# Modulation weights laid out with one output per partition, multiplied and summed by VectorE alone

## The reference

```python
cond = jax.nn.silu(c)                                # first block, c is [1, 1024]
mod = (cond @ ada_w[i] + ada_b[i])[:, None, :]       # 2 layers, ada_w[i] is [1024, 6144]
sh1, sc1, g1, sh2, sc2, g2 = jnp.split(mod, N_MOD, axis=-1)
h = rmsnorm(x, norm_mix_g[i]) * (1.0 + sc1) + sh1
...
mod = (jax.nn.silu(c) @ w_mod[i] + b_mod[i])[:, None, :]         # second block, 2 layers
mod_c = (jax.nn.silu(c_ctx) @ w_mod[i] + b_mod[i])[None, None, :]
```

## Time and profile before

| | |
|---|---|
| median of 3 runs (lowest, highest) | 4114.86 us (4112.88, 4119.44) |
| the profiled execution, its span | 4124.29 us, 4122.5 us |
| mean granted TensorE clock | 0.938 |
| TensorE busy, x matmuls | 3679.5 us (89%), 17052 |
| VectorE busy, x instructions | 1795.2 us (44%), 3111 |
| ScalarE, GpSimd busy | 1292.1 us (31%), 1001.6 us (24%) |

### The profile page before, as it was taken

One profiled execution on the slowest core, in us unless ns is written; L12 is line 12 of the kernel. 1 busy time (PEld: TensorE's weight loads), 2 busy tenths in 40 slices (PEclk: granted clock), 3 DMA queues, 4 the chain that ended last, 5 costly groups with the idle time before them and its releaser, 6 DMA issues. The chain is left out here.

```text
span 4122.5 us, 42200 instructions
## 1 busy us (share of the span) xinstructions
PE 3679.5 (89%) x17052; PEld 2688.1 (65%) x17052; DVE 1795.2 (44%) x3111; ACT 1292.1 (31%) x2282; POOL 1001.6 (24%) x874
## 2 busy tenths in 40 slices
PE   7998999878888898898959988899998989998997
PEld 3446878436467785464658865788886447746885
DVE  7637775275388864412335542312224005322223
ACT  1413222245222223615423323321113335533222
POOL 0223433120033330002025520222222011004443
PEclk8998999989989899999979989999999999999998
DMA  6425543110144431110011111111111111012221
GB/s 268 155 79 194 200 159 142 46 41 1 62 156 181 164 153 72 41 41 21 1 30 42 42 44 41 62 62 62 62 62 41 57 41 46 1 41 82 82 102 62
DMA packets 67042, 333.94 MB, mean 81 GB/s; under 512 B 32352, under 2 KB 35360, under 8 KB 42016
## 3 DMA queue, kind: packets, MB, share of 16 engines
q1 hardware_dynamic: 66416, 328.86, 21.6%
q10 hardware_dynamic: 432, 2.38, 0.1%
HBM read 324.30 MB, written 6.91 MB: 80 GB/s over the span
## 5 line engine op out<-in xcount | busy, mean ns | idle before, releaser
L629 PE MATMUL PSB<-R,R 128*128 128x512 f32 (+1 forms) x2432 | 930.6, 383 | 93.9 <-DVE R L887 48.7
L603 POOL TENSOR_TENSOR R<-SB,R 128x1024 fp32r<-128x1024 f32 x260 | 640.0, 2463 | 1425.6 <-ACT R L594 1425.3
L630 PE MATMUL PSB<-R,R 128*128 128x512 f32 (+1 forms) x2432 | 898.6, 377 | 0.0
L559 PE MATMUL PSB<-SB 128*128 128x512 f32 (+1 forms) x2176 | 847.4, 551 | 23.4 <-ACT SB L1285 18.5
L633 PE MATMUL PSB<-R,R 128*128 128x512 f32 (+1 forms) x2432 | 846.8, 378 | 0.0
L559 PEld LDWEIGHTS PSB<-SB 128*128 128x128 f32 x2176 | 422.1, 195 | 441.9 <-issue 412.1
L629 PEld LDWEIGHTS PSB<-R,R 128*128 128x128 f32 x2432 | 467.7, 192 | 218.7 <-issue 31.7
L630 PEld LDWEIGHTS PSB<-R,R 128*128 128x128 f32 x2432 | 468.1, 192 | 79.7
L633 PEld LDWEIGHTS PSB<-R,R 128*128 128x128 f32 x2432 | 437.7, 193 | 65.8
L421 DVE SCALAR_TENSOR_TENSOR SB<-SB 128x512 f32<-128x512 f32 x504 | 473.7, 984 | 7.2 <-DMA SB<-in_ada 2.0
L594 ACT ACTIVATE R<-SB 128x1024 fp32r<-128x1024 f32 x260 | 273.1, 1052 | 553.8 <-PE PSB L633 535.1
(11 more groups left out here) (320 smaller groups left out, 4132.0 us busy)
## 6 DMA issues: line engine op xcount, KB each, us to landing
SB<-in_w SPq DMA_DIRECT2D x95, 2048.0 KB, 8.5
SB<-in_ada SPq DMA_DIRECT2D x96, 1024.0 KB, 5.1
SB<-gate_rows SPq DMA_DIRECT2D x12, 512.0 KB, 4.5
SB<-in_rpb SPq DMA_DIRECT2D x8, 448.0 KB, 3.4
spill<-SB SPq DMA_DIRECT2D x1, 3072.0 KB, 10.5
SB<-gate_rows SPq DMA_DIRECT2D x24, 128.0 KB, 3.8
SB<-spill SPq DMA_DIRECT2D x1, 3072.0 KB, 9.9
SB<-in_x SPq DMA_DIRECT2D x8, 256.0 KB, 4.7
```

The source lines that it names most:

```text
L559: ins = e.mm(banks[ring[(g + c) % len(ring)]][0:m, 0:n], t[:, 0:m], xs[k][:, lo:lo + n], k == 0, k == nkt - 1)
L603: e.tt(lr, t, hf, ALU.subtract).then_inc(*G.up(("lo", j), *done))
L629: e.mm(b[:, 0:n], wh, xh[:, lo:lo + n], x == 0, False)
L630: e.mm(b[:, 0:n], wh, xl[:, lo:lo + n], False, False)
```

## The change

The weights are packed with one output per partition: a half is [128, 2048] = 2 groups of 128 outputs with all 1024 inputs of each along the free axis. The three condition vectors (`in_cond`, 3 x 1024) are loaded to all 128 partitions as rows of 1024 columns, into the place of constants that only later stages use (`lvF` to `negB`, `cosM`, `sinM`). For each group and condition VectorE issues one `tensor_tensor_reduce`: weights times condition, summed along the row, starting from the bias, the sum written straight to the modulation vector. The full product is written too, over the weights or, for the first of two conditions, into a tile `products`. TensorE has no part in it and the bank is free. silu is now worked out on rows of 1024 columns (two ScalarE passes and one VectorE pass for each condition). The displaced constants are loaded by SyncE in the stage `even`, behind the spill, and four places wait for them. The start value is per partition, a column of the bias.

```diff
-for _n, _w in (("ident", 128), ("bd64", 128), ("rot64", 128), ("rot32", 128),
+for _n, _w in (("lvF", 896), ("lvB", 896), ("cosM", 512), ("sinM", 512),
                ("triF", 128), ("triB", 128), ("negF", 128), ("negB", 128),
...
     def dve(self, v, at, D):
         t = at["t"]
-        if t % 2:
-            self.dve_sums(v, at, D)
...
-        for k in range(4):
-            w = self.slot(t)[:, k * 512:(k + 1) * 512]
-            for x in range(m):
-                c = cond[:, (4 * half + k) * m + x:(4 * half + k) * m + x + 1]
...
-                    v.wait_ge(*self.st.at("acc_part", j, x))
-                    v.stt(acc, w, c, acc, ALU.mult, ALU.add).then_inc(*D.up(*ev))
+        for c in range(2):
+            x = 2 * half + c
+            w = self.slot(t)[:, c * 1024:(c + 1) * 1024]
+            for i, (cond, ready) in enumerate(conds):
+                v.wait_ge(*ready())
+                out, made = (w, []) if i == m - 1 else (self.products, [("products", 2 * t + c)])
+                if made and ("products", 2 * t + c - 1) in D.when:
+                    v.wait_ge(*self.st.at("products", 2 * t + c - 1))
+                v.ttr(out, w, cond, 1.0, bias[:, x:x + 1], ALU.mult, ALU.add, MOD[:, x * m + i:x * m + i + 1]).then_inc(
+                    *D.up(("half", t), ("mod", j), *made))
...
+            def condition(e, i):
+
+                e.wait_ge(cond_landed[i], 16)
+                if i:
+                    e.wait_ge(*st.at("cond", i - 1))
+                e.act(silu, conds[i], ACT.Tanh, scale=0.5).then_inc(*A.up())
+                e.wait_ge(*A.now())
+                e.act(conds[i], conds[i], ACT.Copy, scale=0.5).then_inc(*A.up(("half_cond", i)))
+
...
+                e.load(conds[0], d_cond[0].partition_broadcast(128)).then_inc(cond_landed[0], 16)
+                condition(e, 0)
                 e.wait_ge(x_landed, 128)
-                e.load(cst[:, 0:NORMS], d_const[:, 0:NORMS]).then_inc(const_landed, 16)
+                for i in range(1, 3):
+                    e.load(conds[i], d_cond[i].partition_broadcast(128)).then_inc(cond_landed[i], 16)
+                e.load(cst[:, LATER:NORMS], d_const[:, LATER:NORMS]).then_inc(const_landed, 16)
...
+                for i in range(1, 3):
+                    condition(e, i)
...
+                for i in range(1, 3):
+                    v.wait_ge(*st.at("half_cond", i))
+                    v.stt(conds[i], silu, 1.0, conds[i], ALU.add, ALU.mult).then_inc(*D.up(("cond", i)))
...
                 e.load(spill, XREG).then_inc(spill_landed, 16)
+                e.load(cst[:, 0:LATER], d_const[:, 0:LATER]).then_inc(later_landed, 16)
```

More of the change, by code:

```diff
@@ L337, with __init__ @@
     count = 0
-    def __init__(self, st, jobs, alloc_tiles, bank, d_ada, ones, sems, early=()):
-        self.st, self.jobs, self.bank, self.d_ada, self.ones = st, jobs, bank, d_ada, ones
-        self.sems, self.early = sems, early
+    def __init__(self, st, jobs, alloc_tiles, d_ada, sems, early=()):
+        self.st, self.jobs, self.d_ada, self.sems, self.early = st, jobs, d_ada, sems, early
         self.slots = alloc_tiles(2, 2048)
-        self.accs = [alloc_tiles(2, 512) for _ in range(max(j[2] for j in jobs))]
+        self.products = alloc_tiles(1, 1024)[0] if any(len(j[1]) > 1 for j in jobs) else None
         self.base = Modulation.count - len(early) // 2
@@ L365, in sp @@
             at["t"] += 1
[L367 to L397, removed]
@@ L399, in dve @@
     def dve(self, v, at, D):
         t = at["t"]
[L401 to L403 removed]
         if t >= 2 * len(self.jobs):
             return
+        at["t"] += 1
         j, half = divmod(t, 2)
[L407 removed]
+        _, conds, bias, MOD = self.jobs[j]
+        m = len(conds)
         v.wait_ge(*self.landed(t))
[L409 to L421 removed]
+        for c in range(2):
[8 more added lines that the diff above has]
+                    *D.up(("half", t), ("mod", j), *made))
@@ L663, in rglru @@
             AA = [x[:, 0:S] for x in XB]
-            fill = modulation(st, mod_jobs(0), banks[6],
+            fill = modulation(st, mod_jobs(0),
                               [(SB[:, later + 2048 * i:later + 2048 * (i + 1)], sem(f"ada_early{i}")) for i in range(6)])
+            silu = alloc(1024)
             gs = small(8)
@@ L698, in pe @@
                     e.mm(banks[7], ones, SQ[f % 2], f == 0, f == 7).then_inc(*P.up(("square_sum", f)))
[L699 to L702, removed]
-                g = linear(e, st, 0, ring, "a_in", rows, 8, H, LAT, lambda k, lo: [st.at("h", k)],
-                           each=lambda i: fill.pe(e, at, P))
+                g = linear(e, st, 0, ring, "a_in", rows, 8, H, LAT, lambda k, lo: [st.at("h", k)])
                 for f, name in gates:
-                    if name == "gr":
-                        fill.pe(e, at, P)
                     for k in range(2):
@@ L717, in pe @@
                     g += 1
-                fill.pe_flush(e, at, P)
                 g = linear(e, st, g, ring, "a_in", range(10, 20), 8, H, LAT, lambda k, lo: [])
@@ L792, in dve @@
                     fill.dve(v, at, D)
-                fill.dve_sums(v, at, D)
                 v.wait_ge(*st.at("mod", 3))
@@ L904, in ffn1 @@
             SQ = R
-            fill = modulation(st, mod_jobs(1) + mod_jobs(2, 0, 6) if i == 0 else mod_jobs(2, 6) + mod_jobs(3), banks[6])
+            fill = modulation(st, mod_jobs(1) + mod_jobs(2, 0, 6) if i == 0 else mod_jobs(2, 6) + mod_jobs(3))
             n1, n2 = f"f1_{i}", f"f2_{i}"
@@ L934, in pe @@
                     g = linear3(e, st, g, ring, hv, n1, range(8 * q, 8 * q + 8), range(8), H, LAT,
-                                lambda x, lo: [st.at("h", x)], each=lambda x: x < 7 and fill.pe(e, at, P))
+                                lambda x, lo: [st.at("h", x)])
                     g = linear3(e, st, g, ring, hv, n2, range(8), range(8 * q, 8 * q + 8), HID, LAT,
-                                lambda x, lo: [st.at("hid", q, x)], each=lambda x: x % 2 and fill.pe(e, at, P))
-                fill.pe_flush(e, at, P)
+                                lambda x, lo: [st.at("hid", q, x)])
                 if i == 1:
```

57 lines of the change are left out of this document (29 added, 28 removed).

## The result

| | before | after |
|---|---|---|
| median of four runs each, on the same chip | 4117.15 us | 4048.23 us (4045.99 to 4050.19) |
| span of the profiled execution | 4122.5 | 4045.6 |
| mean granted TensorE clock | 0.938 | 0.944 |
| TensorE busy, x matmuls | 3679.5 us, 17052 | 3594.8 us, 16476 |
| VectorE busy, x instructions | 1795.2 us, 3111 | 1789.4 us, 3062 |

The ratio is 0.9833, 95% interval 0.9816 to 0.985: 69 us faster, where I had forecast 33.

The account below looks back on a forecast made before the run. Bound: TensorE, busy 89% of the span; work counts when it is TensorE's or TensorE waits for it. -22.1 - 7 + 4 + 3 - 11 = -33 us from 4114.86 gives 4081 us; own range 4055 to 4108, 8 in 10 4050 to 4112.

Parts of the forecast that it names:

- column sums and last quarters, ffn1: ffn1 stages: removing TensorE's column sums on the path saves 22.1 us, shorter waits in each stage's last quarter 7 us.
- VectorE's products, ffn1: ffn1 halves on the path: 14 with one condition save 3.8 us, 38 with two cost 7.6; sum +4 us.
- clock: TensorE waits in one piece before the second product of a quarter; 3 us added, between 0 and 10.
- first stage: Start and gates of the first stage together: 11 us less, between 7 and 14.
- VectorE, new price: A VectorE product of 1024 columns costs 1.33 us, bounds 1.25 to 1.45; two conditions gain nothing.
- The panel and the late half: First-stage gates: SyncE reaches the weight panel at about 126 us; the modulation half behind it lands about 138, 11 ahead.
- from there on the gate chain is ScalarE's: First-stage gates: after the late modulation half, ScalarE sets the pace, so the stage gains 11 us, start included.
- GpSimd's hold: Modulation halves in ffn1: GpSimd still holds one VectorE instruction in each half, for about 2.0 us.
- the moved constants: 1.7 MB of constants loaded on SyncE's queue behind the spill: no cost; uncovered, some 11 us once.
- Half rate: VectorE's product runs at half rate, some 2.4 us each: about 4330 us in all; chance 10%.
- Gain absorbed: GpSimd holds VectorE again in the square behind 16 of 52 halves, costing 32 us: 4107 to 4118 us; chance 7%.
- Product not held: VectorE's product escapes holding by GpSimd, 52 halves times 2 us go: some 3980 us; chance 5%.

Follow-up runs that it names:

- the two runs over all stages: Changed kernel with as many 1-column matmuls put back on constants: 4086.34 us; kernel before without TensorE's column sums, its multiply-adds kept: 4075.83 us.
- the order alone: Kernel before with the 36 modulation halves of each ffn1 stage spread nine to a quarter instead of 11, 11, 11 and 3, column sums kept: 4055.58 us.
- the run with pieces: Changed kernel with each product of 1024 columns cut into two of 512, each with its own accumulator read: 4079.11 us.

## Why the prediction was wrong in size

| term | forecast | measured |
|---|---|---|
| column sums and last quarters, ffn1 | -29.1 | -32.4 (kernel before without them) |
| VectorE's products, ffn1 | +4 | -19.8 (changed kernel less that one, clock included) |
| clock | +3 | in the line above; 0.94 to 0.96 and 0.91 to 0.93 |
| first stage | -11 | -17.9 |
| sum | -33 | -70, medians -69 |

**The step that failed is "VectorE, new price".** I took 1.33 us a product, with 1.25 as the lower bound; it is 1.21. I summed 0.67 (the read's start), 0.54 (512 more columns) and 0.12 (to the next instruction). The first two are right to the hundredth: 0.67 + 0.54 = 1.21. The 0.12 isn't VectorE's time but the wait of a dependent instruction: with that wait put between the products they start 1.33 us apart, and the run is 20 us slower (a part of it by the wait in front of each half, which my sum doesn't have). Over some 180 products in the ffn1 stages the 0.12 makes 22 us, and +4 less 22 is -18. The bound was wrong for the same reason: I let only a part of the 0.12 go, where a row with an independent successor would have let all of it go. So two conditions gain as well, some 0.25 us a half (5.1 less 4 x 1.21), and the sentence that they gain nothing fell. That sentence rested on the right reading, that the two interleaved sums of the old form hid each other's wait; I didn't see that the products, which don't need each other either, would hide theirs.

My range, 4055 to 4108 us, also isn't the sum of the bounds that stand beside it: with the other terms as forecast they add up to 4060 to 4114 us. The measured time lies outside either.

**The first stage** was mis-sized by 7 us. The panel and the late half were right. The start came out near (X from 37.30, said 38), but by luck: VectorE waited for weights until 27.06 us, where I had no wait after 21.8, and the cheaper product made up for it. The step "from there on the gate chain is ScalarE's" was wrong. Before, a column sum that waited for VectorE held TensorE in front of the last 24 gate matmuls (until 157.50 us), and the rest of the stage is TensorE's; without it TensorE is through the gates 18.5 us earlier. Taking out the sums alone gives 13.4 of the 17.9 us.

**Right:** the sums that count and their price (29.1 against 32.4, with the +38 and -42 us of the two runs over all stages); that GpSimd's hold stays; the second product of a quarter at 5.44 us a row (line 984 at 369.05 and 374.49 us with one condition, 10.88 for two rows from 1162.18 with two); that the moved constants cost nothing that can be seen (by the profile they give a few us at the start, which I had at nothing). The price of the new silu no run separates.

**The rivals.** *Half rate*: refuted. The Trainium skill, Vector Engine (DVE) Microarchitecture Reference, Points that are easy to get wrong, would have both fp32 inputs in SBUF halve the throughput; this trace doesn't agree for this instruction: 1.28 us for 1024 columns with the sum, and 1.27 in the form with one input in PSUM. *Gain absorbed*: GpSimd's subtraction did get longer (mean 2463 to 2622 ns), and TensorE's waits for it became its largest (57.4 us over the span), so it may have taken a part of the gain. But the squares behind a half stay at 0.68 us, and the gain is larger than forecast; only squares of rows without a half are held, 14 of 64 in the ffn1 stages against 8 before. *Product not held*: false for the changed kernel, true for the form with a PSUM input, where it gave 47 us.

## What to carry to other kernels

Read the price of an instruction from a pair whose second doesn't need the first's result; the start-to-start time of a dependent pair contains a wait that an independent stream doesn't pay (here 0.12 us of 1.33). Where one engine is the bound only in part of a repeated stretch, spread its extra work over the stretch before making it cheaper: here the order alone gave as much as the new instructions. And where VectorE and GpSimd both read SBUF, moving one input of VectorE's instruction to PSUM took the hold off that instruction (none of 120 held).

## What the runs showed of the hardware that I had not expected

- The accumulator read costs next to nothing in a stream of independent products, as the next one starts with it: 0.67 us from start to start for 512 columns, against 0.66 for line 421's multiply-adds with two conditions, which have no read. For 1024 columns it is 1.21 us; a successor that waits for the sum starts 0.12 later.
- A product with one input in PSUM is as fast as with both in SBUF (medians 1274 and 1280 ns) and in 120 was never held by GpSimd (maximum 1283 against 3461 ns).
- GpSimd's hold doesn't grow with the instruction that it meets: some 2.1 us on a product of 512 columns (2.88 us instead of 0.74 in the run with pieces) as on one of 1024 (3.42 instead of 1.28), and 1.8 us on the square.
